# A two-block transformer kernel: the recurrent mixer's decays as products instead of exponentials of sums

## What is computed

```python
def gates(f_raw, lb):                       # lb: lower bound per key channel
    f = lb + (1.0 - lb) * sigmoid(z)        # share that the state keeps
    return (1.0 - lb) * sigmoid(-z), log(f) # key, log of the decay
# S_t = exp(log_f_t) * S_{t-1} + k_t v_t^T,   o_t = S_t^T q_t
o_f = recurrence(qh, k_f, vh, lf_f)                     # forwards
o_b = flip(recurrence(flip(qh), flip(k_b), flip(vh), flip(lf_b)))
o = rms_norm(o_f + o_b, out_norm_w) * silu(g)
```

## Time and profile before

| | |
|---|---|
| median of 3 runs | 1650.57 us (1650.04 to 1650.74) |
| profiled execution | 1649.89 us, its span 1648.1 us |
| busy over the span | PE 88%, DVE 54%, ACT 45%, POOL 3% |
| DMA | 400.16 MB, mean 243 GB/s |
| PE's mean granted clock | 0.96 of full |

### The profile page before, as it was taken

The page is one execution under the profiler, slowest core; times in us unless marked ns, Lnnn a source line. Parts: engine busy times, 40 slices in busy tenths (PEclk is TensorE's granted clock), DMA queues, the critical chain, the costliest instruction groups (busy, mean ns, idle before and its releaser), DMA issues.

```text
span 1648.1 us, 23732 instructions
## 1 busy us (share of the span) xinstructions
PE 1442.5 (88%) x9288; PEld 1086.6 (66%) x9288; DVE 886.9 (54%) x1198; ACT 746.8 (45%) x864; POOL 47.0 (3%) x38
## 2 busy tenths in 40 slices
PE   7996878766666666899999999999999999999998
PEld 7895732211111111688889878888888889888887
DVE  4679642121211212576666767666766666766665
ACT  5564233222122221555554755444755454764443
POOL 0006300000000000000000000000000000000000
PEclk9998979899898999899999999999999999999999
DMA  7632499999999999765555336554656546346552
GB/s 233 187 103 73 182 424 426 428 427 429 429 428 428 429 427 428 248 213 194 179 178 179 129 128 205 192 190 153 206 180 196 185 137 213 111 154 204 184 197 76
DMA packets 164071, 400.16 MB, mean 243 GB/s; under 512 B 5752, under 2 KB 136232, under 8 KB 151592
## 3 DMA queue, kind: packets, MB, share of 16 engines
q1 hardware_dynamic: 162824, 397.74, 65.7%
q10 hardware_dynamic: 1184, 1.57, 0.3%
HBM read 398.23 MB, written 1.06 MB: 242 GB/s over the span
## 4 chain that ended last, share of the span: by engine, by line
PE 61%; DMA 26%; DVE 6%; ACT 4%; issue 2%; POOL 0%; SPq 0%; ACTq 0%; DVEq 0%; POOLq 0%
PE ps L946 20%; PE ps L948 10%; DMA ring<-w_expert_gate 8%; DMA ring<-w_expert_up 8%; PE ps L627 6%; DMA ring<-w_expert_down 6%; PE ps L629 6%; PE ps L628 6%; PE ps L847 2%; PE ps L602 2%; PE ps L603 2%; PE ps L604 2%; DMA ring<-w_in 2%; DMA raw_sb<-ffn_gate 1%; ACT w1h_sb L1190 1%
## 5 line engine op out<-in xcount | busy, mean ns | idle before, releaser
L946 PE MATMUL ps<-xT_both,wh_sb 128*128 128x512 f32 x1408 | 501.4, 400 | 4.1 <-DVE xT_both L1545 4.1
L1878 DVE TENSOR_TENSOR wl_sb<-raw_sb,wh_sb 128x2048 fp32r<-128x2048 f32 x162 | 371.1, 2292 | 169.7 <-ACT wh_sb L1333 169.5
L948 PE MATMUL ps<-xT_both,wl_sb 128*128 128x256 f32 x1408 | 395.9, 281 | 0.0
L1333 ACT ACTIVATE wh_sb<-raw_sb 128x2048 fp32r<-128x2048 f32 x162 | 309.0, 1909 | 60.3 <-PE ps L604 53.3
L946 PEld LDWEIGHTS ps<-xT_both,wh_sb 128*128 128x128 f32 x1408 | 265.3, 188 | 71.0 <-DVE xT_both L1545 5.2
L948 PEld LDWEIGHTS ps<-xT_both,wl_sb 128*128 128x128 f32 x1408 | 266.8, 189 | 1.4
L847 PE MATMUL ps<-ring,work 128*32 128x512 f32 x928 | 124.1, 661 | 62.3 <-DMA ring<-w_expert_up 31.6
L1855 DVE COPY work<-ps 128x512 f32<-128x512 f32 x32 | 33.0, 1071 | 240.8 <-PE ps L847 240.8
L627 PE MATMUL ps<-wh_sb,hidh_sb 128*128 128x512 f32 x384 | 152.0, 396 | 1.2 <-DVE wl_sb L1878 1.2
L1343 ACT ACTIVATE xT_sb<-ps 128x512 f32<-128x512 f32 x88 | 52.5, 597 | 217.6 <-PE ps L948 217.6
L629 PE MATMUL ps<-wh_sb,hidl_sb 128*128 128x512 f32 x384 | 150.2, 391 | 0.0
(11 more groups left out here) (319 smaller groups left out, 2079.4 us busy)
## 6 DMA issues: line engine op xcount, KB each, us to landing
raw_sb<-ffn_gate SPq DMA_DIRECT2D x44, 1024.0 KB, 5.4
raw_sb<-ffn_up SPq DMA_DIRECT2D x44, 1024.0 KB, 5.4
raw_sb<-ffn_down SPq DMA_DIRECT2D x44, 1024.0 KB, 4.8
ring<-w_expert_gate SPq DMA_DIRECT2D x20, 2048.0 KB, 45.7
ring<-w_expert_down SPq DMA_DIRECT2D x20, 2048.0 KB, 46.1
ring<-w_expert_up SPq DMA_DIRECT2D x18, 2048.0 KB, 46.3
work<-w_expert_up SPq DMA_DIRECT2D x11, 2048.0 KB, 45.0
raw_sb<-w_in SPq DMA_DIRECT2D x22, 1024.0 KB, 5.4
```

What stands on the lines that cost most here:

```text
L946: pe.matmul(bank(2 * r + n).rearrange("p (m s) -> p m s", m=2), w_h[:, k, fs], xT_hl[:, :, k, :], start=k == 0, stop=False, skip_group_che ...
L948: mm = pe.matmul(bank(2 * r + n)[:, 0:S], w_l[:, k, fs], xTh[:, k, :], start=False, stop=k == KD - 1, skip_group_check=True)
L1333: nc.scalar.activation(wh[j], raw[j], ACT.Copy).then_inc(sem["w_hi"], 1)
L1878: dve.tensor_tensor(wl[j], raw[j], wh[j].bitcast(F32), ALU.subtract).then_inc(raw_free[j], 1)
```

## The change

Levels are now built from small to large. Level 0 is the diagonal, levels 1 to 7 are w = 1, 2, ... 64, level 8 is w = 128. ACT turns the gates into decay factors (`factors`, four 128x256 instructions for each direction), and no logarithm, sum or exponential is taken. The decay of q and k at a level is that of the level below, times the total decay of the neighbouring small block where it has to be crossed: kf, kb and q_place are multiplied in place, step by step. POOL multiplies pairs of totals up to blocks of 64 (`tot_done`), and extends the backward keys (128x512); DVE extends the forward keys (`extend_key`, 128x512) and q for both directions (`extend_q`, 128x1024, in place, once PE has read it for the level before). ACT copies the halves of kf and kb that a level needs into one operand (`merge`). PE reads q from q_place by runs of w columns, alternating between the two directions' halves (`crossed`). The results of levels 1 to 5 and the diagonal are put by DVE with masks; levels 6, 7 and 8 by ACT, by strips of partitions (`far_put`). `half_proj` is half a projection, of one tile of 128 tokens; one stands between any two levels from 0 to 6. `project1(0)` moves behind the recurrence, split 16 from POOL to DVE, and split 17 behind all of POOL's key products. Half 0 of the experts waits for level 3's operands in place of the last's, but it stands behind the last piece of w_out in SP's order; half 1 waits for the matmuls of level 8.

The diff, cut to its core:

```diff
+        forget, key_sum, tot_pairs = r1(2 * HH * S), r1(HH * S), r1(HH * S)
+        q_place = r1(2 * HH * S)
...
+        merged = [a_place[:, HH * S * i:HH * S * i + HH * S] for i in range(2)]
+        BACKWARD, FORWARD = 0, 1
+        totals, tot_at = {1: forget, 2: tot_pairs}, 0
+        for v in (4, 8, 16, 32, 64):
+            totals[v] = tot_high[:, tot_at:tot_at + 2 * HH * S // v]
+            tot_at += 2 * HH * S // v
+
+        def total(d, v):
+
+            return totals[v][:, d * HH * S // v:(d + 1) * HH * S // v].rearrange("p (n f) -> p n f", f=2)
+
+        def crossed(place, w, start, n):
+
+            return bass.AP(place.tensor, place.offset + start, [place.ap[0], [2 * w, n], [HH * S + w, 2], [1, w]])
...
-            sp.wait_ge(sem["lev_q"], NLEV)
-            sp.wait_ge(sem["lev_k"], NLEV)
+            sp.wait_ge(sem["lev_q"], 3)
+            sp.wait_ge(sem["lev_k"], 3)
             half(0, 0, 0)
-            sp.wait_ge(sem["lev_put"], NLEV + 1)
+            sp.wait_ge(sem["lev_ps"], NLEV + 1)
+            sp.wait_ge(sem["lev_put"], NEAR)
             half(1, 0, 1)
...
+            def half_proj(p, t):
+
+                o, i = p // 2, p % 2
+                w = parts1(p)
...
+                mm = tokens3(Z_BANK[o], FS * i, w, (x1h, x1l), tiles=[t])
+                if t == TT - 1:
+                    mm.then_inc(sem["z_ready"], 1)
 
             def level(i):
 
-                pe.wait_ge(sem["lev_k"], i + 1)
-                if i < NLEV:
-                    pe.wait_ge(sem["lev_q"], i + 1)
+                w = 1 << i >> 1
+                if i in (0, NLEV):
+                    pe.wait_ge(sem["lev_k"], max(i, 1))
+                else:
+                    pe.wait_ge(sem["merged"], i)
+                if i:
+                    pe.wait_ge(sem["lev_q"], i)
...
                 elif i == 1:
                     pe.wait_ge(sem["eT_dve"], NG // 2)
                     pe.wait_ge(sem["o_put"], TT)
+                elif i < NLEV:
+                    pe.wait_ge(sem["lev_put"], i - 1)
                 else:
-                    pe.wait_ge(sem["lev_put"], i - 1)
-                moving = q_l[i % 2] if i < NLEV else hq
+                    pe.wait_ge(sem["k_scaled"], NLEV + 1)
+                    pe.wait_ge(sem["far_put"], 1)
                 for h in range(HH):
                     for t in range(TT):
-                        to = 1 - t if i == 0 else t
+                        at_k, at_q = h * S + t * P, h * S + (1 - t) * P
+                        if i == 0:
+                            k, q = key_sum[:, at_k:at_k + P], hq[:, h, t * P:t * P + P]
+                        elif i < NLEV:
+                            k, q = merged[i % 2][:, at_k:at_k + P], crossed(q_place, w, at_k, P // (2 * w))
+                        else:
+                            k = key_place[:, HH * S * t + at_k:HH * S * t + at_k + P]
+                            q = q_place[:, HH * S * (1 - t) + at_q:HH * S * (1 - t) + at_q + P]
                         c = (h % 2) * S + t * P
-                        mm = pe.matmul(bank(2 * (i % 2) + h // 2)[:, c:c + P], k_l[i % 2][:, h, t * P:t * P + P],
-                                       moving[:, h, to * P:to * P + P], start=True, stop=True)
+                        mm = pe.matmul(bank(2 * (i % 2) + h // 2)[:, c:c + P], k, q, start=True, stop=True)
...
-                pe.wait_ge(sem["lev_put"], NLEV + 1)
+                pe.wait_ge(sem["lev_put"], NEAR)
+                pe.wait_ge(sem["far_put"], 3)
...
-            for i in range(3):
-                proj(13 + i)
-                level(i)
+            level(0)
+            for i in range(6):
+                half_proj(13 + i // 2, i % 2)
+                level(i + 1)
             pe.wait_ge(sem["z_hi"], 1)
             turn_mixed(4, 0)
-            level(3)
+            level(7)
             pe.wait_ge(sem["z_hg"], 1)
             pe.wait_ge(sem["xT_lo"], 6)
-            residual(range(TT))
-            level(4)
+            residual([0])
+            level(8)
+            residual([1])
+            recurrence()
             project1(0)
-            level(5)
-            for i in range(6, NLEV + 1):
-                level(i)
-            recurrence()
             project1(1)
...
-            def decay(i):
-                act.wait_ge(sem["lev_sub"], i + 1)
-                nc.scalar.activation(lev_e[i % 2], lev_e[i % 2], ACT.Exp).then_inc(sem["lev_exp"], 1)
+            def forget_of(d):
+                return forget[:, (1 - d) * HH * S:(2 - d) * HH * S]
+
+            def factors(d):
+
+                act.wait_ge(sem["lb_ready"], 3)
+                act.wait_ge(sem["factors"], 2 * d + 1)
+                for h in range(HH):
+                    i, f = d * HH + h, forget_of(d)[:, h * S:h * S + S]
+                    a = nc.scalar.activation(f, f, ACT.Identity, scale=oml[:, i:i + 1], bias=lb[:, i:i + 1])
+                a.then_inc(sem["factors"], 1)
+
+            def merge(i):
+
+                w = 1 << i >> 1
+                act.wait_ge(sem["k_scaled"], i + 1)
+                act.wait_ge(sem["lev_k"], i)
+                if i == 1:
+                    act.wait_ge(sem["o_ps"], TT)
+                else:
+                    act.wait_ge(sem["lev_ps"], i - 1)
+                for f, k in enumerate((kf, kb)):
+                    to, of = [a.rearrange("p (n f w) -> p n f w", f=2, w=w)[:, :, f, :]
+                              for a in (merged[i % 2], k.rearrange("p h s -> p (h s)"))]
+                    a = nc.scalar.activation(to, of, ACT.Copy)
+                a.then_inc(sem["merged"], 1)
+
+            def far_put(i):
+
+                act.wait_ge(sem["lev_ps"], i + 1)
+                act.wait_ge(sem["lev_put"], NEAR)
+                if i == NLEV:
+                    nc.scalar.activation(at_off.rearrange("p h t c -> p (h t c)"), bank(0, 2), ACT.Copy).then_inc(sem["far_put"], 1)
+                    return
+                w = 1 << i >> 1
+                crossing = bank(2 * (i % 2), 2).rearrange("p (n c) -> p n c", c=P)
+                for r in range(P // w):
+                    rows, cols = slice(r * w, r * w + w), slice((r ^ 1) * w, (r ^ 1) * w + w)
+                    a = nc.scalar.activation(at_diag.rearrange("p h t c -> p (h t) c")[rows, :, cols], crossing[rows, :, cols], ACT.Copy)
+                a.then_inc(sem["far_put"], 1)
...
-            logs()
+            factors(1)
...
-            decay(0)
+            merge(1)
             hi1(15)
-            decay(1)
-            decay(2)
+            merge(2)
             hi1(16)
-            decay(3)
+            merge(3)
+            merge(4)
             hi1(17)
-            decay(4)
+            merge(5)
+            merge(6)
             act.wait_ge(sem["z_ready"], 16)
             nc.scalar.activation(gs_tok.rearrange("p t n -> p (t n)"), bank(Z_BANK[7], 2), ACT.Silu).then_inc(sem["z_hg"], 1)
+            merge(7)
+            far_put(6)
             hi_mixed(4, 0)
-            for i in range(5, NLEV):
-                decay(i)
+            far_put(7)
+            far_put(8)
             hi1(18)
...
+            def first_q():
+
+                dve.wait_ge(sem["factors"], 4)
+                dve.wait_ge(sem["z_hq"], 1)
+                dve.tensor_tensor(q_place.rearrange("p (x n) -> p x n", x=2), forget.rearrange("p (x n) -> p x n", x=2),
+                                  hq.rearrange("p h s -> p (h s)").unsqueeze(1).to_broadcast([P, 2, HH * S]), ALU.mult)\
+                    .then_inc(sem["lev_q"], 1)
+
+            def extend_key(i):
+
+
+                v = 1 << i >> 2
+                n = HH * S // (2 * v)
+                dve.wait_ge(sem["merged"], i - 1)
+                if v > 1:
+                    dve.wait_ge(sem["tot_done"], v.bit_length() - 1)
+                first = kf.rearrange("p h s -> p (h s)").rearrange("p (n f w) -> p n f w", n=n, f=2)[:, :, 0, :]
+                dve.tensor_tensor(first, first, total(FORWARD, v)[:, :, 1:2].to_broadcast([P, n, v]), ALU.mult).then_inc(sem["k_scaled"], 1)
+
+            def extend_q(i):
+
+
+                v = 1 << i >> 2
+                n = HH * S // (2 * v)
+                dve.wait_ge(sem["lev_ps"], i)
+                q, t = crossed(q_place, v, 0, n), totals[v]
+                opposite = bass.AP(t.tensor, t.offset + 1, [t.ap[0], [2, n], [HH * S // v - 1, 2], [0, v]])
+                dve.tensor_tensor(q, q, opposite, ALU.mult).then_inc(sem["lev_q"], 1)
 
             def put(i):
 
                 dve.wait_ge(sem["lev_ps"], i + 1)
...
+                if i:
                     dve.wait_ge(sem["lev_put"], i)
...
+                dve.wait_ge(sem["mask_in"], 32)
+                mask = masks[:, 7 - i, :].bitcast(U32).unsqueeze(1).to_broadcast([P, HH * TT, P])
+                dve.copy_predicated(at_diag.rearrange("p h t c -> p (h t) c"), mask,
+                                    bank(2 * (i % 2), 2).rearrange("p (n c) -> p n c", c=P)).then_inc(sem["lev_put"], 1)
...
             copy_eT(NG - 1)
```

(57 more changed lines are left out.)

109 lines of the change are left out of this document (16 added, 93 removed).

## The result

The changed kernel took **1628.83 us** (median of 4 runs, 1627.32 to 1630.47), the kernel before it 1650.65 beside it (1650.04 to 1651.53): a ratio of **0.9869 [0.9857, 0.9881]**, 21.8 us less by the medians. The two profiled executions, 1649.89 and 1630.47, are 19.4 apart. Two further measurements of the same kernel in later sessions gave 0.9889 [0.9873, 0.9904] (median 1630.6) and 0.9873 [0.9856, 0.9889] (1629.77). In the first of these one of the five executions took 7811.63 us and is left out; it was the profiled one, so that measurement has no trace here. The forecast was 1630.6.

A forecast was written before the change was run, and what follows sets the result against it. DVE was taken to bound the mixers' tail, DMA the experts and PE the rest. The turning 19.1 us earlier plus 0.9 from DMA gave 20.0, so 1630.6 from a median of 1650.57; range 1628 to 1634.

The forecast's parts named there:

- signs of being wrong: Wrong if a small-w level lasts over 2, PE waits for DVE or ACT each level, or first reuse hasn't moved 19.
- Factors: On ACT: four Identity take 2.0, first set ahead of split 11 delays PE by 2.0, net +1.0 at the last turning.
- The cover at the other end: The 4.0 us between tile 11's projection and the last turning of weights shrink to 3.0, hiding part of the second factors.
- Levels: PE bounds the stage: six times half a projection (2.87) plus a level (1.80), 4.67 each; level 7 ends at 153.8.
- Level matmuls at 1.8 whatever w: Expected in the profile: PE's level matmuls keep 1.8 us although q's columns alternate between two places.
- zero and double: Extra cost of PE's alternating operand at w=1: taken as 0; if that level doubled, the sum would be 18.2, not 20.0.
- DVE stays the bound: Rival: DVE waits for POOL's six products, 4.9 to 7.5 us longer, about 1636; chance 0.22, shared with dearer prices.
- The last level: After level 7, POOL's split 17 delays DVE's q 8 to 159.7; level 8 ends at 161.6, residual(1) at 163.3.
- Q first: Rival: DVE asks for q 8 before POOL starts split 17, level 8 starts at 156.7 not 159.8: 1627.5; chance 0.20.
- residual(1): ... at full clock: PE after level 8: residual(1) taken at full clock, 1.7, where both residuals took 5.65 after long idle; ends at 163.3.
- The turning of the mixed heads: On PE after recurrence and both project1 parts: at 178.3 instead of 197.41, 19.1 us earlier.
- DMA: First slot reuse moves from 236.6 to 217.5, queue dry for 5 us at no cost, 0.9 more gained.

The follow-up runs named there:

- halves late: Changed kernel with the experts' halves 0 and 1 also waiting for the recurrence's output: 1633.92 us, ratio 0.9908 to the kernel before.
- whole projections: Changed kernel with whole projections 13, 14, 15 ahead of levels 1, 2, 3 and levels 3 to 6 back to back: 1638.54 us, ratio 0.9931.
- q first: Changed kernel with POOL's split 17 waiting for the q of level 8; run twice: 1625.73 us (ratio 0.9855) and 1627.24 us (0.9859).
- factors late: Changed kernel with the first four factors moved from ahead of split 11 to behind the last exponentials: 1626.4 us, ratio 0.9861.
- w=1 contiguous: Changed kernel with PE reading q at w=1 as contiguous columns of one direction, altering part of the computation: 1629.17 us, ratio 0.9877.
- more DVE: Changed kernel with DVE also copying the results of levels 1 to 5 to an unread place: 1631.84 us, ratio 0.9883.
- cover back: Changed kernel with both residuals and project1(0) on PE between levels 7 and 8 again: 1628.99 us, ratio 0.9873.
- both repairs: Changed kernel with the first factors behind the last exponentials and POOL's split 17 behind q 8: 1625.24 us, ratio 0.985.
- half 0 early: As both repairs, with the experts' half 0 issued ahead of the last piece of w_out: 1625.67 us, ratio 0.9852.

## Why the prediction was right

The time was 1628.8 to 1630.6 for a forecast of 1630.6, by the forecast mechanism: DVE gave up the bound, PE runs half, level, half, level, and the reuse of the slots moves with it. Part of the agreement is luck, though: two of the prediction's own signs of being wrong came true, as a level at small w lasted over 2 (2.81 at w=1, 2.09 at w=2) and the first reuse moved by 15.7 and not by 19. Two other terms made up for most of the difference. Step by step:

- **Factors.** Predicted +2.0 for the first set and a net +1.0 at the last turning of weights. The first set cost 1.96. The cover at the other end held: the last two turnings are 1.39 us apart (113.27, 114.66), 2.28 before (109.74, 112.02). From the first turning to the last, the same front took 38.8 to 40.4 us in nine traces (the middle one 39.5), +0.9 to +2.4 over before's 37.9; the profiled execution of the changed kernel is near the upper end with 40.2. So the forecast of +1.0 is at the lower end, and what the term leaves out is PE's clock, which came up later (below).
- **Levels.** 4.6 to 4.75 apart, 4.67 predicted, with a clock of 1.00 from 135 to 158. "Level matmuls at 1.8 whatever w" was wrong by 0.85 us for w=1 and 0.14 for w=2. Of the two numbers weighed for w=1, zero and double, the truth was half-way: 0.85 of 1.8.
- **DVE stays the bound** (a rival). It didn't: 19.1 of 23 us busy (135 to 158), and some 6 us more of it cost only 2.
- **The last level.** Predicted: POOL's split goes first, the q ends at 159.7 and level 8 at 161.6. Measured: the q ended at 161.4, since level 7 came 2.6 later than forecast and everything moved, and it was 4.33 long, as forecast in kind; level 8 ended at 164.8. The rival "Q first" was real as a mechanism and worth 3.1 by its working: forced, it came 2.5 us lower beside the changed kernel. In the changed kernel it did not happen, POOL starting 1.7 us ahead of DVE's request.
- **Level 8's clock.** Not foreseen. After the idle time PE's clock fell (0.57 from 162 to 166), and level 8 and the residual took 1.65 more. The step that failed here is "residual(1): ... at full clock".
- **The turning of the mixed heads**, the sum's main term: 15.9 in place of 19.1. The 3.2 are 1.6 of the front, 0.85 of w=1, and 1.65 of the clock at level 8, less some 0.9 where POOL's split came sooner after level 7.
- **DMA.** 0.9 predicted between the reuse and the end of the experts (237.4 less 236.60 is 0.8), 1.6 measured (15.7 at the reuse, 17.3 at the second block's weights). The queue was dry near 218 to 221, where 212 to 217 was forecast. Late halves cost 5.4 us of the stage, which confirms that the early ones carry the gain past it. Where the 0.7 over the forecast comes from was not looked into.
- **A term that was missing.** The second block gave 2 more, 17.3 to 19.4. Of these 1.5 lie in its first 30 us, where PE's clock came up sooner than in the profile of before (28.1 us against 29.6 from the second block's weights to the load two further). By 15.9 + 1.6 + 2.0 the sum comes to 19.5, against the 20.0 predicted: one term too high by 3.2, one too low by 0.7, one of 2.0 not there. That these nearly cancel is the luck.

## What to carry to other kernels

When an engine is freed from being the bound, put the work that covers the new chain between its links, in halves if need be: whole projections between the levels cost 6.7 us in the stage by the trace, and 9.7 by the medians, of a gain of 21.8. A two-input DVE instruction that follows closely behind a long POOL one on SBUF data should be ordered by hand when PE waits for it: losing the race cost 4.1 us in the trace here, and a wait of one line on POOL wins it. And a gain ahead of a DMA-bound stage arrives in full only if the transfers that fill its buffers move forward too (5.4 us of the stage here); one half moved further still bought nothing.

## What the runs showed that was not expected

**The granted clock makes or loses 1 to 1.7 us at three places**, in executions whose code there is the same. All of it lies in windows where PE has just worked again after idle time.

At the front, the clock's rise between 75 and 90 us. The windows of the changed kernel (columns of the earlier trace rows; the third last number is the clock):

```profile
80.00:85.00 5.00, 5.00 (x19) 4.17 (x20) 3.66 (x7) 0.91 (x2) 0.00 (x0) 0.50 0.00 0
85.00:90.00 5.00, 5.00 (x37) 5.00 (x36) 1.47 (x9) 0.00 (x0) 0.00 (x0) 0.80 0.70 207
```

With q first (its first trace), whose front is the same code, these two windows had 0.73 and 1.00; the kernel before had 0.79 and 1.00, its PE busy the whole 10 us as well. The changed kernel's projections ran at half speed for longer, 1.4 us to the last turning of weights. A part of this is the change's own doing: with late factors this first window has 0.69 to 0.85, as said above. The rest is between executions of one code (0.50 to 0.73 in the first window).

At level 8, the idle time before was 2.25 or 2.26 us in five traces. In three of them (the changed kernel twice, w=1 contiguous) the clock fell, and from level 8 to the recurrence it took 5.2 us; in two (factors late, halves late) it stayed, and it took 3.58. It also stayed after 1.81 us (more DVE) and 1.96 (whole projections). This is the row of the one with the factors late, to be held against 161.51 and 3.25 above:

```profile
157.41 2.02 PE L703 MATMUL ps<-ring,work 128*128 128x128 f32 x16 [2.25 <-issue]
```

At the start of the second block's feed-forward, the 15 us after its first weights, in the changed kernel (windows again):

```profile
655.59:670.59 15.00, 14.17 (x81) 12.28 (x80) 10.32 (x20) 11.59 (x21) 1.89 (x1) 0.95 0.66 222
```

With the cover back:

```profile
652.76:667.76 15.00, 14.70 (x69) 12.17 (x68) 10.26 (x19) 10.96 (x19) 1.90 (x1) 0.79 0.67 232
```

The clock here is 0.93 to 0.96 in six traces (the changed kernel in both, factors late, the first q first, whole projections, w=1 contiguous) and 0.73 to 0.79 in seven (before, cover back, the second q first, both repairs, half 0 early, halves late, more DVE). From this load of weights to the gate's load two further it takes 28.1 to 28.3 us in the six and 29.0 to 30.4 in the seven. That is how the gains of 3.2 and 4.8 us in the last table came down to 2.3 and 2.6 at the end, and it is 1.5 of the 2.0 that the prediction's sum had missing. What decides it was not tried; a profile of one execution is uncertain by as much for this kernel, and steps under 2 us are better read as distances within a trace than from its end.

**Identity cost no table load here.** Both sets of factors ran on ACT straight after instructions of another function, and the exponentials after the first set, with no load between, 2.06 us for four; the prediction's bound of 1.3 for a load was not needed.
